# Sample rows' attention placed inside the last 17 steps of the prompt's main attention, in a hybrid NSA + GLA decoder step on one core

## The reference

```python
(q, kv, gate, z_a, q_g, k_g, v_g, a_low, z_b, merge) = split(rms_norm(x) @ w_in)
# attention (NSA): 8 query heads in 2 groups, three branches, each its own softmax
o_nsa = gate[0] * attend(q, compressed k, v) + gate[1] * attend(q, selected k, v) + gate[2] * attend(q, window k, v)
# gated linear attention (GLA): 4 heads, decay from log_sigmoid(a_low @ a_up + a_b)
o_g = gla_chunked(q_g, k_g, v_g, log_a, state)
y = x + (sigmoid(g_a) * (o_nsa * silu(z_a) @ w_ba) + sigmoid(g_b) * (norm(o_g) * silu(z_b) @ w_bb)) @ w_out
```

## Time and profile before

| what | us |
|---|---|
| median of 3 runs | 1400.13 (1395.86 to 1402.26) |
| the profiled execution, its own time | 1407.33 |
| its span, first to last instruction | 1405.3 |
| TensorE busy over the span | 1324.4 (94%) |
| VectorE, ScalarE busy | 613.7, 621.4 (44% each) |
| first transposes of the main attention to the end of the last | 409.5 to 984.4 |
| from there to the first matmul of the GLA core | 984.4 to 1039.8 |

### The profile page before, as it was taken

How to read it: one execution, slowest core, us unless ns; L and a number is a source line. 1 busy time by engine, 2 the same in 40 slices (tenths; PEclk the granted TensorE clock), 3 DMA queues, 4 the chain that set the end, 5 groups by cost and what they waited for, 6 DMA issues and landing times.

```text
span 1405.3 us, 23475 instructions
## 1 busy us (share of the span) xinstructions
PE 1324.4 (94%) x9533; PEld 1190.3 (85%) x9533; DVE 613.7 (44%) x1365; ACT 621.4 (44%) x1063; POOL 148.5 (11%) x182
## 2 busy tenths in 40 slices
PE   5999989998989999999999999999778889999998
PEld 4999989998978889988888899889556678999876
DVE  5211145634733344434333333332489766453342
ACT  5212235442332555655565567564558542221121
POOL 2100001103200000000000000001710270000000
PEclk9999999999989999999999999999779999999999
DMA  7251453411212212212122112212645555443231
GB/s 199 63 170 33 138 118 91 128 51 59 67 36 56 62 57 62 63 56 62 57 77 62 48 56 61 73 42 67 232 154 191 198 174 177 153 139 104 90 127 60
DMA packets 141307, 137.38 MB, mean 98 GB/s; under 512 B 27121, under 2 KB 125761, under 8 KB 141137
## 3 DMA queue, kind: packets, MB, share of 16 engines
q1 hardware_dynamic: 138416, 127.47, 29.8%
q0 software_dynamic: 2784, 8.43, 2.1%
HBM read 98.02 MB, written 41.88 MB: 100 GB/s over the span
## 4 chain that ended last, share of the span: by engine, by line
PE 65%; DVE 4%; ACT 2%; issue 2%; POOL 1%; DMA 1%; another core or an unknown queue 0%; POOLq 0%; SPq 0%; DVEq 0%; ACTq 0%
PE ps L218 37%; PE ps L2285 6%; PE ps L1176 5%; PE ps L1210 5%; PE ps L1192 4%; PE ps L1225 1%; PE ps L2196 1%; POOL oL L2334 1%; PE ps L2176 1%; DVE S L2392 1%; PE ps L2200 1%; PE ps L2293 1%; PE ps L1146 0%; DVE sP L1361 0%
## 5 line engine op out<-in xcount | busy, mean ns | idle before, releaser
L218 PE MATMUL ps<-hH,wH 128*128 128x352 f32 (+1 forms) x1320 | 443.0, 336 | 7.9 <-ACT stg L334 4.9
L218 PE MATMUL ps<-hH,wL 128*128 128x352 f32 (+1 forms) x1320 | 428.2, 324 | 0.0
L218 PE MATMUL ps<-hL,wH 128*128 128x352 f32 (+1 forms) x1320 | 427.5, 324 | 0.0
L218 PEld LDWEIGHTS ps<-hH,wH 128*128 128x128 f32 (+1 forms) x1320 | 250.0, 189 | 38.3 <-issue 26.9
L218 PEld LDWEIGHTS ps<-hL,wH 128*128 128x128 f32 (+1 forms) x1320 | 251.0, 190 | 2.2 <-issue 1.9
L218 PEld LDWEIGHTS ps<-hH,wL 128*128 128x128 f32 (+1 forms) x1320 | 250.0, 189 | 0.3
L1361 DVE CUSTOM_DVE_ANT_0 sP<-ps,dist,stat 128x256 f32<-128x256 f32 (+3 forms) x116 | 58.5, 542 | 203.4 <-issue 132.2
L205 DVE TENSOR_TENSOR wL<-w_raw,wH 128x1024 fp32r<-128x1024 f32 (+1 forms) x55 | 67.8, 1233 | 162.0 <-ACT wH L197 162.0
L1429 ACT ACTIVATE pPT<-ps 128x512 f32<-128x512 f32 x74 | 44.1, 596 | 181.2 <-PE ps L1192 181.1
L334 ACT ACTIVATE stg<-ps 128x352 f32<-128x352 f32 x132 | 60.8, 462 | 98.5 <-PE ps L218 90.0
L1472 ACT ACTIVATE sP<-sP,stat 128x640 f32<-128x640 f32 (+7 forms) x128 | 93.0, 729 | 4.4 <-DVE stat L1361 3.8
(11 more groups left out here) (378 smaller groups left out, 2100.8 us busy)
## 6 DMA issues: line engine op xcount, KB each, us to landing
w_raw<-in_w_in SPq DMA_DIRECT2D x46, 512.0 KB, 3.9
p_spill<-stg SPq DMA_DIRECT2D x132, 176.0 KB, 1.8
zt<-p_spill SPq DMA_DIRECT2D x24, 528.0 KB, 5.0
w_raw<-in_w_in SPq DMA_DIRECT2D x17, 256.0 KB, 3.8
gvT<-p_spill SPq DMA_DIRECT2D x8, 528.0 KB, 6.6
rq<-p_spill SPq DMA_DIRECT2D x8, 528.0 KB, 6.2
x_all<-in_x_prompt SPq DMA_DIRECT2D x8, 512.0 KB, 9.6
m_raw<-in_w_branch_b SPq DMA_DIRECT2D x8, 512.0 KB, 5.5
```

Source lines behind the costliest of these rows:

```text
L218: mm = nc.tensor.matmul(ps[0:t.m, bank, 0:NF], w[:, c % 2, t.m * k:t.m * k + t.m], x[:, k, NF * n:NF * n + NF], start=(k == 0 and i == 0), ...
```

## The change

The sample rows' attention and the head of the GLA part are moved from their own stage into the main attention's steps.

- The 93 units are dealt out over the first 49 steps (`M0` = 49) in place of 66; the last 17 steps have none. Below t = m - 49 is the number of a step among these, 0 to 16.
- The two compressed parts run earlier, beside the units: scores in steps 12 and 19, probability turn and values two steps later. They borrow spare columns of the units' banks 2 and 3 (`borrow`), and a later unit that wants the bank waits until they are read (`held`).
- The other four parts use banks 2 and 3 in the last 17 steps: scores at the end of t = 2, 6, 10, 14, score on VectorE and exponential at t = 3, 7, 11, 15, turn and values at t = 4, 8, 12, 16. The page turns stand behind the step's own `transposes` (table `TURNS`); the decay gates stand ahead of or at the end of steps 0, 7, 11 and 15.
- In these steps VectorE's order is: sample score, copy of sample probabilities, `copies` with `drain`, `output`, `weigh`, `score(m+3)`, and a piece of the GLA head (`head_part`). ScalarE's is: `probs`, gate evictions, `copies` with key copies and the spread copy, sample exponential, and its pieces of the GLA head.
- The biases of the sample rows are built by GpSimd ahead of step 49, in one set instead of two. Head 0's values are turned inside `core(0)`, behind its first products. `rq`, `eb` and `reset` have two copies; `gvT` of head 1 and `rq` of head 1 are loaded after the last `o_added`.

```diff
@@ -322,6 +323,8 @@
                     pe.wait_ge(sem("w_low"), c + 1)
                 if u >= 2:
                     unit_out(pe, u - 2)
+                if u in held:
+                    pe.wait_ge(sem(held[u][0]), held[u][1])
                 ring.products(c, n, bank, hH, hL).then_inc(sem("u_done"), 1)
         def act_units(act, count=1):
...
         def units_at(m):
+            return UA * (m + 1) // M0 - UA * m // M0 if m < M0 else 0
...
+        M0 = 49
+        C_AT = (12, 19)
+        TURNS = {1: (1, 2), 2: (3,), 3: (4,), 5: (5, 6), 6: (7,), 7: (8,), 9: (9, 10), 10: (11,), 11: (12,), 13: (13, 14),
+                 14: (15,)}
...
+        def borrow(pe, what, u, read):
+            last = unit["pe"] - (1 if what == "scores" else 2)
+            unit_out(pe, last)
+            held[last + 2] = (read, u + 1)
+            lent[what, u] = 3 - last % 2
+            return lent[what, u]
...
+            def turn_page(c):
+                n, b = divmod(c, NB)
+                if b == 0:
+                    pe.wait_ge(sem(f"kp_loaded{n % 2}"), 16 * NB * (n // 2 + 1))
+                    if n >= 1:
+                        pe.wait_ge(sem("z_scored"), n + 2)
+                elif b == 1:
+                    pe.wait_ge(sem("kpT_copied"), c)
+                    if n >= 1:
+                        pe.wait_ge(sem("zPT_copied"), n + 2)
+                elif b == 2:
+                    if n == 0:
+                        pe.wait_ge(sem("zl_copied"), 1)
+                    else:
+                        pe.wait_ge(sem("z_out"), n + 2)
+                else:
+                    pe.wait_ge(sem("kpT_copied"), c - 1)
+                for j in range(4):
+                    mm = nc.tensor.transpose(ps[:, page_bank(c), P * j:P * j + P], kp[n % 2][:, b, P * j:P * j + P],
+                                             ident[:, :])
+                mm.then_inc(sem("kpT_done"), 1)
...
+            def before_step(t):
+                if t == 0:
+                    unit_out(pe, NU - 2)
+                    unit_out(pe, NU - 1)
+                    decay_gate(pe, 0, 0)
+                    decay_gate(pe, 0, 1)
+                if t in (7, 11, 15):
+                    pe.wait_ge(sem("z_scored"), t // 4 + 3)
+                    decay_gate(pe, *((1, 0), (1, 2), (2, 1))[t // 4 - 1])
+                if value_unit(t):
+                    turn_probs(value_unit(t))
+            def after_step(t):
+                if t == 0:
+                    pe.wait_ge(sem("zl_part"), 1)
+                    decay_gate(pe, 0, 2)
+                    pe.wait_ge(sem("zl_part"), 2)
+                    turn_page(0)
+                if t == 7:
+                    pe.wait_ge(sem("zl_part"), 3)
+                    decay_gate(pe, 1, 1)
+                if t == 11:
                     pe.wait_ge(sem("zl_copied"), 2)
-                    turn_v(pe, 0, 4)
-                elif u == 4:
-                    pe.wait_ge(sem("gv_copied"), NV)
-                    gates(pe, 2)
+                    decay_gate(pe, 2, 0)
+                if t == 15:
+                    pe.wait_ge(sem("zl_part"), 6)
+                    decay_gate(pe, 2, 2)
+                if score_unit(t):
+                    z_scores(score_unit(t))
...
+                t = m - M0
+                pe_units(pe, units_at(m))
+                if m - 2 in C_AT:
+                    turn_probs(C_AT.index(m - 2))
+                before_step(t)
+                transposes(m)
+                for c in TURNS.get(t, ()):
+                    turn_page(c)
+                if m >= 1:
+                    values(m - 1)
+                if m - 2 in C_AT:
+                    z_values(C_AT.index(m - 2))
+                if value_unit(t):
+                    z_values(value_unit(t))
+                if m + LA < ncut:
+                    scores(m + LA)
+                if m in C_AT:
+                    z_scores(C_AT.index(m))
+                after_step(t)
+                for j in closed(m - 1):
+                    spread(j)
+            values(ncut - 1)
+            spread(4 * R - 1)
...
+            def head_part(t):
+                if t == 1:
+                    minus_abs(dve, 0)
+                elif t == 5:
+                    log_sigmoid(dve, link, 0)
+                elif t == 6:
+                    sums(dve, 0)
+                elif t == 7:
+                    tails(dve, link, 0)
+                elif t == 9:
+                    queries(dve, link, 0)
+                elif t == 10:
+                    inverses(dve, 0)
+                elif t == 11:
+                    keys(dve, link, 0)
+                elif t == 13:
+                    spans(dve, link, 0)
+                    for n in range(NSTG):
+                        dve.wait_ge(sem(f"p_stored{n}"), 16 * ((NU - n + NSTG - 1) // NSTG))
+                elif t == 14:
+                    later_queries(link, 0)
+                elif t == 15:
+                    minus_abs(dve, 1)
...
+            def tail_step(m):
+                t = m - M0
+                if t % 4 == 3:
+                    z_score(score_unit(t - 1))
+                if value_unit(t):
+                    copy_probs(value_unit(t))
+                copies(m)
+                if value_unit(t):
+                    output(value_unit(t))
+                for j in range(4 * R):
+                    if cut_of[4 * j + 3, 0] == m:
+                        weigh(j)
+                if m + LA < ncut:
+                    score(m + LA)
+                head_part(t)
...
+            def tail_step(m):
+                t = m - M0
+                if t == 0:
+                    gate_out(act, 0, 0)
+                    gate_out(act, 0, 1)
+                if t in (7, 11, 15):
+                    gate_out(act, *((1, 0), (1, 2), (2, 1))[t // 4 - 1])
+                copies(m)
+                if t == 0:
+                    gate_out(act, 0, 2)
+                    copy_key(0)
+                if t % 4 == 3:
+                    z_probs(score_unit(t - 1))
+                if t == 3:
+                    log1p(act, 0)
+                elif t == 7:
+                    gate_out(act, 1, 1)
+                elif t == 8:
+                    exps(act, 0)
+                elif t == 9:
+                    tail_exps(act, 0)
+                elif t == 11:
+                    gate_out(act, 2, 0)
+                elif t == 15:
+                    gate_out(act, 2, 2)
+                elif t == 16:
+                    log1p(act, 1)
...
         def _(sp):
-            sp.dma_start(o_spill[:, R - 1, :], oTn[:, R - 1, :]).then_inc(sem("o_spilled"), 16)
-            for n in range(NSTG):
-                sp.wait_ge(sem(f"p_stored{n}"), 16 * ((NU - n + NSTG - 1) // NSTG))
-            load_v(sp, 0)
-            fetch_pages(sp, 1, "k", kp[1][:, :, :])
-            load_qk(sp, 0)
-            fetch_pages(sp, 1, "v", vp[:, 1, :, :])
+            sp.wait_ge(sem("aup_zero"), 1)
+            for r0 in (0, 64, 96):
+                sp.dma_start(aupR[r0:r0 + RANK, :], a["gla_alpha_up"][0]).then_inc(sem("aup_loaded"), 16)
+            for r in range(R - 1):
+                sp_units(sp, 39 + UA * min(M0, last_cut(16 * r + 15) + 5) // M0 - unit["sp"])
+                if r == R - 2:
+                    sp.wait_ge(sem("u_done"), NU)
+                    fetch_pages(sp, 1, "k", kp[1][:, :, :])
+                    load_qk(sp, 0)
+                    fetch_pages(sp, 1, "v", vp[:, 1, :, :])
+                sp.wait_ge(sem("o_added"), 4 * r + 4)
+                sp.dma_start(o_spill[:, r, :], oTn[:, r, :]).then_inc(sem("o_spilled"), 16)
             fetch_pages(sp, 3, "k", kp[1][:, :, :])
             fetch_pages(sp, 3, "v", vp[:, 1, :, :])
-            sp.wait_ge(sem("o_spilled"), 16 * R)
+            sp.wait_ge(sem("z_out"), 4)
+            sp.dma_start(orow_spill[0:NB].rearrange("b x t d -> (b x t) d"), orow[:, 0, :]).then_inc(sem("orow_spilled"), 16)
+            load_v(sp, 0)
+            sp.wait_ge(sem("o_added"), 4 * R)
+            sp.dma_start(o_spill[:, R - 1, :], oTn[:, R - 1, :]).then_inc(sem("o_spilled"), 16)
             load_v(sp, 1)
             load_qk(sp, 1)
-            for gp in range(2):
-                sp.wait_ge(sem("z_out"), max(u for u, unit in enumerate(ZU) if unit[0] == gp) + 1)
-                sp.dma_start(orow_spill[NB * gp:NB * gp + NB].rearrange("b x t d -> (b x t) d"), orow[:, gp, :])\
-                    .then_inc(sem("orow_spilled"), 16)
+            sp.wait_ge(sem("z_out"), len(ZU))
+            sp.dma_start(orow_spill[NB:DB].rearrange("b x t d -> (b x t) d"), orow[:, 1, :]).then_inc(sem("orow_spilled"), 16)
```

More of the change, by code:

```diff
@@ new lines, in turned @@
+        def turned(act, h, j):
+            act.wait_ge(sem("gv_done"), NV * h + j + 1)
+            if h == 0 and j < 2:
+                act.wait_ge(sem("o_added"), 4 * R - 1 + j)
+            bank = value_bank(h, j)
+            if j < 4:
+                ins = nc.scalar.activation(vh[h % 2][:, 2 * j:2 * j + 2, :],
```

(23 more changed lines are left out.)

1018 lines of the change are left out of this document (474 added, 544 removed).

## The result

The changed kernel takes 1447.1 us (median of 4, 1446.1 to 1450.6) against 1398.4 of before in the same rounds: ratio 1.035, 95% interval 1.032 to 1.038. It is slower by some 49 us, forecast were 24, in a range up to 1444. The direction was right and the size was half. The profiled execution took 1450.6 us, span 1448.9.

A forecast was written before the change was run, and what follows sets the result against it. TensorE bounds the main attention, a chain across engines the sample stage. Tail +3.4, compressed parts +12.4, GLA core +2.5 and clock +5 sum to 23.3 on the profiled 1407.3; with the median 7.2 lower, forecast 1424, range 1400 to 1444.

The forecast's parts named there:

- The compressed parts, +12.4: Steps 12 to 14 and 19 to 21: added TensorE work plus two unit waits, 6.2 us each part, +12.4 together.
- The two waits that I had walked: Units held by each compressed part: one waits 1.6 us for the part's score, another 3.3 us for output.
- The clock, +5: Last 17 steps: TensorE's clock drops with thinner work, costing +5 us, bounds 0 and +21.5.
- the clock falls in the tail: Rival, 16%: TensorE stays at clock 0.77 over all 17 last steps, 21.5 us in place of 5, 1440.
- The stops of the tail, 33.5: Last 17 steps: TensorE's waits on chains through VectorE and ScalarE, listed step by step, sum to 33.5 us.
- the one at t = 7: From t = 6 to 7 the gate on TensorE waits for the sample score on VectorE, 6.5 us.
- The `log1p` stop: From t = 3 to 4, ScalarE's log1p with two table loads delays the exponentials the next transposes need, 4.7 us.
- TensorE's work there, 72.0: Last 17 steps: all TensorE work without units sums to 72.0 us, 4.2 us a step.
- The GLA core, +2.5: GLA core: head 0's value turns and copies no longer hide, and loads come late, +2.5 us, bounds 0 and 5.
- The late loads: GLA core: head 1's rq and gvT, asked for after the last o_added, come 0 to 3 us late.
- The first rival: Rival, 13%: TensorE's work bounds the tail, 8 us of stops remain, -13.5 in all, 1387.

The follow-up runs named there:

- early_free: Changed kernel with the compressed parts' scores and values placed behind the units so that no unit waits for them: 1.013 of before.
- early_spread: early_free with the eight short VectorE instructions that build the sample queries dealt one to a step over steps 2 to 9: 1.015 of before.
- fill: Changed kernel with 100 unneeded identity transposes where TensorE stops in the last 17 steps: 1.028 of before; repeated unaltered as fill_again, 1.032.
- drain_last: Changed kernel with VectorE, in the last 17 steps, doing score(m+3) and the sample score ahead of the drain: 1.022 of before.
- combo2: early_spread, drain_last and loads_early together, plus head 0's log1p one step later and step 48's VectorE copy ahead of weigh: 1.001 of before.
- combo4: combo3 with 48 identity transposes to an idle bank, in the tail and ahead of two value turns in the core: 0.998 of before.
- combo3: combo2 with the spread-weight copy behind the next exponentials and page turns ahead of transposes at t = 10, 13: 0.998 of before; repeated as combo3_again, 0.998.
- loads_early: Changed kernel with gvT and rq of head 1 loaded ahead of the wait for the last o_added: 1.033 of before.
- after: The changed kernel itself, unaltered, against the kernel before: 1447.1 us, 1.035.
- before_stops: Kernel before, with TensorE waiting at the end of eight steps until the last issued unit is out of its bank: 1424.6 against 1405.7 us, 1.015.

## Why the prediction was half of it

**The compressed parts, +12.4: this step failed.** The term was 9.8 of waits and 2.6 of work; measured are 24.3 of waits and of slow work behind them (early_free), and 1.3 of their own work. The two waits that I had walked were right to .2 us. Two things were not in the term: the wait of the scores for the unit just issued, 6.2 us, which stands in `borrow` (`1 if what == "scores" else 2`) and which I had overlooked; and the slow matmuls behind the stops, 8.8. Outside the term stood the sample queries in step 9, 3.5 us with their slow stretch (early_spread), a move that I gave no price at all. (24.3, 1.3 and 3.5 sum to 29.1 and not to the +25.0 of the table. The 523.3 of before holds all of its own 2.6 us of stops, and its units take TensorE 1.6 us longer than those of early_spread, which goes over from a step's work to units 49 times and not 66.)

**The clock, +5: too small, and in one place of three.** In the tail it cost TensorE 10 us of its own time (86.2 busy at 0.88 to the end of the last `transposes`, 76 at full speed), and part of these were on the path: fill_again gave back 5.6 at clock 0.96, fill 2.5 at 0.94. I weighed it only there, where the work becomes thin. It cost as much again in the dense stretch, where I had taken the clock for granted: single stops of 3 us between units at full speed, most of them followed by a stretch at a mean of 0.8 to 0.9. The third place is the opening of the core. The rival "the clock falls in the tail" decides under 0.85, and it was 0.89; it did not come true, but its mechanism did, elsewhere.

**The stops of the tail, 33.5: right as a sum, in part by luck.** Measured are 123.33 - 91.79 = 31.5, the one at t = 7 6.18 for 6.5. But some 4.4 of the 31.5 were not in my list, and those that were came to 27. The 3.85 ahead of the second half of step 49's `transposes` was missing: in step 48 VectorE's copy stands behind `weigh`, which waits for exponentials. The `log1p` stop was 2.81 for 4.7, and 4.12 once the slow work ahead of it had gone. On ScalarE `log1p` itself took from 984.84 to 989.62, 4.78 for 4.81 before:

```profile
984.84 1.07 ACT L1396 ACTIVATE ls<-ls 128x1056 f32<-128x1056 f32 x1
985.92 1.28 ACT L1398 ACT_TABLE_LOAD   x1
987.22 1.08 ACT L1398 ACTIVATE ls<-ls 128x1056 f32<-128x1056 f32 x1
988.32 1.28 ACT L2122 ACT_TABLE_LOAD   x1
989.62 0.72 ACT L2122 ACTIVATE sP<-sP,stat 128x512 f32<-128x512 f32 x1
```

Both loads are 1.30 from start to the next activation, so the 2.66 for a switch that the Trainium skill gives (ScalarE: Activation LUTs, What ACT_TABLE_LOAD costs) did not show here either. Three orders on VectorE and ScalarE (drain_last, and the two of combo2) made 18 of the tail's 123 us.

**TensorE's work there, 72.0: some 4 too low,** by the 76 above. The sample values are 1.01 + .35 us each with the new keys' part, and a gate at full clock takes .26 to .36 from start to start, both more than I took; they are about half of the 4. With that the tail adds up: to the end of the last `transposes` 110.5 forecast, less 2.0 of stops, 3.9 more work and 5.3 more at the slow clock make the 117.7 measured.

**The GLA core, +2.5: 4.6 measured, the cause right in part.** All of it lies in the opening. Head 0's value turns stand there now, with stops of 1.8 and 1.6 us for ScalarE's copies, and behind them TensorE runs slow: with the stops filled the opening is 3.1 shorter (combo4 against combo3_again). The late loads that I had given up to 3 us made about .8 (loads_early). The clock was not in this term.

**The first rival,** a tail bound by TensorE's work (86 us), did not come true: even combo3's is some 15 us longer.

## What to carry to other kernels

Price a borrowed or shared buffer at every place that takes it, the first too, and price what a stop does to the engine's clock where the work is dense, not only where it is thin: here 15.5 us of waits between full-speed units cost 24.3. When work is moved off a stage in which no engine is full into a loop whose filler it displaces, the order on the other engines has to be laid anew for the loop without filler: the same work went from +3.5% to -0.2% by its place and order alone. Forecast the order as written, and look for the instruction that waits at the head of a queue with ready work behind it. And look for a stop that you removed one step further on: half of `log1p`'s stood there.

## What the hardware showed that I had not expected

Stops of TensorE of 2.5 to 3.6 us amid 99% busy stretches were in 8 of 10 cases (after, before_stops and early_free together) followed by microseconds at 1.2 GHz (a mean of 0.79 to 0.90 of full speed over the next 15 us), and in 2 (2.81 and 3.13 us) by none. The same five stops at the same instructions, in fill, had other slow stretches behind them than in after, and one of them none. And work that nobody needs made a kernel faster: 100 added transposes, 4.8 us off the median.
